# The second norm of a two-layer mixer kernel, taken segment by segment with its inverse roots as columns

## The chip, the core and the metric

The kernel runs on one core of one Trainium2 chip. The metric is the device time of one launch in microseconds (us). The core has TensorE (PE, matrix products into the eight PSUM banks; PEld is its weight load), VectorE (DVE), ScalarE (ACT), GpSimd (POOL) and SyncE (SP), which here issues all DMAs. The engines run their own instruction streams in order and meet at semaphores.

## The reference

Two layers over 512 tokens of width 2048: 256 context tokens and 256 latent tokens, whose modulation differs. Layer 0 is a gated chunk mixer with attention, layer 1 a gated delta rule in both directions. What the change touches is the residual of layer 0 and the norm of layer 1, cut to this:

```python
x = x + gate * o                    # latent tokens, layer 0
ctx = ctx + c_gate * oc             # context tokens, layer 0
h = rms_norm(x, norm_w[1]) * (1.0 + scale) + shift
hc = rms_norm(ctx, norm_w[1]) * (1.0 + c_scale) + c_shift
# rms_norm(x, w) = x * rsqrt(mean(x * x, axis=-1) + EPS) * w
qkv, z, ba = split(h @ dn_w_in)     # first products of layer 1
```

## The kernel before

Tokens lie along the free dimension: T = 512 columns, of which segment 0 (columns 0 to 255) is the context and segment 1 (256 to 511) the latent tokens. The model width is 16 k-tiles of 128 partitions. Every large product is made in fp32 quality from three fp32r products: operands are split into a rounded high part and the rest (hh and hl for the activations, wh and wl for the weights), and each k-tile takes hh x wh, hl x wh and hh x wl. Weights come in halves of 8 k-tiles (128x1024). ScalarE makes a half's high part, GpSimd its low part; SyncE loads it into one of six ring slots (layer 0, `ring`, of which the first four are `raw`) or four slots (layer 1, `raw`).

**Last output of layer 0.** PE makes 16 output tiles t (`front_tile`, L695 to L697, halves HOUT + 2t and HOUT + 2t + 1, 48 matmuls of 512 columns each) into banks 0, 1, 3, 4. DVE adds the residual for each segment (L1970, semaphore `x1_ready`), ACT squares the tile (L1346, `square`) and POOL adds the squares into `n_acc` (L2365). Tile 15 goes the same way as the others; PE then waits for POOL's last add and multiplies by a matrix of ones (`square_sum`, L679), which puts the sum over the width of each token into all 128 partitions of bank 6.

**Second norm.** ACT takes the root of 128x512 (L1350), DVE the reciprocal of 128x512 (L1814). Then DVE, ACT and DVE again work through the 16 k-tiles: scale by the inverse root (`norm_scale`, L1819, both inputs in SBUF), affine with the modulation (`norm_affine`, L1361, one operation for each segment), rounding copy to hh (`norm_hi`, L1368), and the rest to hl (`norm_lo`, L1823, both inputs in SBUF). DVE's order is scale(k), lo(k-2); ACT's is affine(k), copy(k-1). ACT makes the high parts of weight halves 0, 1 and 2 of layer 1 (`rear_split_hi`, L474) between root and first affine; POOL makes the low parts (L479) from there.

**First products of layer 1.** PE waits for both parts of weight halves 0 and 1, then for each k-tile 0 to 7 of hl makes six matmuls (halves 0 and 1, banks 0 and 4), then three for each k-tile 8 to 15 (half 2), then needs half 3 (L878 to L880). SyncE issues the loads of halves 0 and 1 when all splits of layer 0 are done, and those of 2 and later after it has sent the latent part of x to memory (`keep_x1`, L554), which waits for the last residual.

The order of the work is written out by hand on each engine; nothing is scheduled by a planner. The names that the change touches are `square_sum`, `norm_root`, `norm_inverse`, `norm_scale`, `norm_affine`, `norm_hi`, `norm_lo`, `products`, `front_half` and the split helpers.

## Time and profile before

| what | us |
|---|---|
| median of 3 runs | 2442.44 |
| lowest, highest | 2440.26, 2444.56 |
| the profiled execution | 2444.82 |
| its span on the core | 2443.0 |
| PE busy | 2337.6 (96%) |
| DVE, ACT, POOL busy | 1101.1, 1128.0, 1162.0 (45%, 46%, 48%) |

The page of the profile gives busy time by engine, the span in 40 slices, the chain of work that ended last, and the costliest groups. Times in the rows are counted from the start of the span. A matmul's duration in a row includes the drain of the array and overlaps the next one's, so what a stretch costs PE is read from the distance between starts. The granted clock (PEclk) is a share of TensorE's 2.4 GHz.

### The profile page before, as it was taken

The numbers are of one execution on the slowest core, as the hardware profiler recorded it, in microseconds if no ns is written. First come the engines' busy times: TensorE is split into PE (matmuls) and PEld (weight loads), VectorE is DVE, ScalarE is ACT, GpSimd is POOL, SyncE is SP. The second block draws the span as 40 slices with busy tenths as digits, with TensorE's granted clock in tenths as the row PEclk, the third lists the DMA queues.
The fourth block names the chain that finished last, engine by engine and source line by source line (L and its number), as shares of the span: only waits on it lengthen the run. The fifth ranks groups of instructions, "written<-read, shape, count | busy, mean of one in ns | idle before, by whom it ended". The sixth has DMA issues, their size and how long they took to land.

```text
span 2443.0 us, 59204 instructions
## 1 busy us (share of the span) xinstructions
PE 2337.6 (96%) x25854; PEld 1944.1 (80%) x25854; DVE 1101.1 (45%) x2337; ACT 1128.0 (46%) x2042; POOL 1162.0 (48%) x634
## 2 busy tenths in 40 slices
PE   6989999999999978999999999999999999998997
PEld 2557777777777856788888888888888888888997
DVE  3144443333440037655555555555555555553323
ACT  3342333323342237554665456545664466543443
POOL 2222333333335544456645664476546654563554
PEclk9999999999999989999999999999999999999998
DMA  9854555555544221233223232323222322336553
GB/s 376 318 201 178 211 212 189 190 193 190 192 181 153 95 95 45 97 114 105 97 89 109 107 108 80 106 105 113 82 103 97 119 100 81 113 103 234 187 181 117
DMA packets 99347, 352.15 MB, mean 144 GB/s; under 512 B 10768, under 2 KB 15248, under 8 KB 96784
## 3 DMA queue, kind: packets, MB, share of 16 engines
q1 hardware_dynamic: 99088, 348.36, 39.7%
q8 instruction: 204, 3.34, 0.6%
q14 instruction: 55, 0.45, 0.1%
HBM read 336.13 MB, written 12.19 MB: 143 GB/s over the span
## 4 chain that ended last, share of the span: by engine, by line
PE 82%; ACT 8%; DVE 4%; DMA 3%; issue 2%; POOL 1%; SPq 0%; ACTq 0%; DVEq 0%
PE bank L695 8%; PE bank L696 8%; PE bank L697 8%; PE bank L878 7%; PE bank L880 6%; PE bank L879 6%; PE bank L652 3%; ACT scratch L1577 3%; PE bank L918 3%; PE bank L920 2%; PE bank L919 2%; PE bank L1118 2%; PE bank L1120 2%; PE bank L1119 2%; PE bank L975 2%; PE bank L1087 2%
## 5 line engine op out<-in xcount | busy, mean ns | idle before, releaser
L479 POOL TENSOR_TENSOR wl<-raw,wh 128x1024 fp32r<-128x1024 f32 x215 | 516.6, 2410 | 623.2 <-ACT wh L474 623.2
L878 PE MATMUL bank<-hh,wh 128*128 128x512 f32 (+1 forms) x1040 | 406.8, 391 | 19.7 <-DVE hl L1823 14.9
L407 POOL TENSOR_TENSOR wl<-raw,wh 128x1024 fp32r<-128x1024 f32 x85 | 207.9, 2455 | 406.4 <-ACT wh L402 406.3
L880 PE MATMUL bank<-hh,wl 128*128 128x512 f32 (+1 forms) x1040 | 381.1, 366 | 1.1 <-issue 1.1
L879 PE MATMUL bank<-hl,wh 128*128 128x512 f32 (+1 forms) x1040 | 380.4, 366 | 1.8 <-issue 1.8
L474 ACT ACTIVATE wh<-raw 128x1024 fp32r<-128x1024 f32 x232 | 245.5, 1060 | 277.9 <-PE bank L920 121.5
L695 PE MATMUL bank<-hh,wh 128*128 128x512 f32 x864 | 346.0, 400 | 2.6 <-POOL wl L407 2.5
L697 PE MATMUL bank<-hh,wl 128*128 128x512 f32 x864 | 338.2, 391 | 0.0
L696 PE MATMUL bank<-hl,wh 128*128 128x512 f32 x864 | 338.1, 391 | 0.0
L878 PEld LDWEIGHTS bank<-hh,wh 128*128 128x128 f32 x1040 | 197.0, 189 | 55.7 <-issue 15.2
L402 ACT ACTIVATE wh<-raw 128x1024 fp32r<-128x1024 f32 x85 | 90.0, 1060 | 311.5 <-DMA raw<-w_in 191.6
L880 PEld LDWEIGHTS bank<-hh,wl 128*128 128x128 f32 x1040 | 196.9, 189 | 35.3 <-issue 2.4
L879 PEld LDWEIGHTS bank<-hl,wh 128*128 128x128 f32 x1040 | 197.7, 190 | 26.5 <-issue 1.0
L695 PEld LDWEIGHTS bank<-hh,wh 128*128 128x128 f32 x864 | 163.4, 189 | 46.0 <-issue 6.9
L696 PEld LDWEIGHTS bank<-hl,wh 128*128 128x128 f32 x864 | 163.4, 189 | 34.9 <-issue 1.9
L697 PEld LDWEIGHTS bank<-hh,wl 128*128 128x128 f32 x864 | 163.2, 189 | 34.8
L2020 DVE SCALAR_TENSOR_TENSOR scratch<-bank,sm,scratch 128x508 f32<-128x508 f32 (+3 forms) x256 | 174.0, 680 | 7.5
L918 PE MATMUL bank<-wh,hh 128*128 128x256 f32 x512 | 158.2, 309 | 3.1 <-issue 3.1
L407 POOL TENSOR_TENSOR wl<-scratch,wh 128x1024 fp32r<-128x1024 f32 x35 | 85.2, 2443 | 138.8 <-ACT wh L402 138.7
L920 PE MATMUL bank<-wh,hl 128*128 128x256 f32 x512 | 145.8, 285 | 0.0
L919 PE MATMUL bank<-wl,hh 128*128 128x256 f32 x512 | 145.6, 284 | 0.0
L975 PEld LDWEIGHTS bank<-scratch 32*32 32x32 f32 x10240 | 105.1, 104 | 33.7 <-issue 27.4
(299 smaller groups left out, 4534.0 us busy)
## 6 DMA issues: line engine op xcount, KB each, us to landing
raw<-w_in SPq DMA_DIRECT2D x259, 512.0 KB, 3.5
raw<-w_ada SPq DMA_DIRECT2D x101, 512.0 KB, 5.6
raw<-w_out SPq DMA_DIRECT2D x84, 512.0 KB, 3.6
scratch<-w_ada SPq DMA_DIRECT2D x59, 512.0 KB, 6.0
scratch<-keep_g SPq DMA_DIRECT2D x15, 1024.0 KB, 5.6
scratch<-w_in SPq DMA_DIRECT2D x23, 512.0 KB, 6.8
raw<-w_gate SPq DMA_DIRECT2D x22, 512.0 KB, 4.6
scratch<-xT SPq DMA_DIRECT2D x2, 4096.0 KB, 12.8
```

What stands on the lines that cost most here:

```text
L407: eng.tensor_tensor(fl[h % SPLIT], ring[ring_slot("half", h)], fh[h % SPLIT].bitcast(F32), ALU.subtract)\
L474: eng.activation(buffers(s)[0], raw[:, s % RAW, :], ACT.Copy).then_inc(sem("rear_hi"), 1)
L479: eng.tensor_tensor(buffers(s)[1], raw[:, s % RAW, :], buffers(s)[0].bitcast(F32), ALU.subtract)\
L695: pe.matmul(ps, w[:, k * P:(k + 1) * P], hhv[:, kk, :], start=first and k == 0, stop=False)
L696: pe.matmul(ps, w[:, k * P:(k + 1) * P], hlv[:, kk, :], start=False, stop=False)
L697: done = pe.matmul(ps, r[:, k * P:(k + 1) * P], hhv[:, kk, :], start=False, stop=last and k == HALF - 1)
L878: pe.matmul(ps, w[:, k * P:(k + 1) * P], hhv[:, kk, t0:t1], start=first and k == k0, stop=False)
L879: pe.matmul(ps, w[:, k * P:(k + 1) * P], hlv[:, kk, t0:t1], start=False, stop=False)
L880: done = pe.matmul(ps, r[:, k * P:(k + 1) * P], hhv[:, kk, t0:t1], start=False, stop=last and k == k1 - 1)
L918: pe.matmul(ps, hhv[:, k, t0:t0 + P], wk, start=(k == 0 and tt == 0), stop=False)
L919: pe.matmul(ps, hhv[:, k, t0:t0 + P], rk, start=False, stop=False)
L920: done = pe.matmul(ps, hlv[:, k, t0:t0 + P], wk, start=False, stop=(k == KT - 1 and tt == 1))
```

## The change

The last output tile, the sum of squares, the norm and the products of k-tiles 0 to 7 and 8 to 15 behind it are made for segment 0 first and for segment 1 after.

- PE makes tile 15 as 48 matmuls of 256 columns for segment 0 (bank 4) and 48 for segment 1 (bank 2). Half NHALF0 - 2 has buffers of its own (`xh`, `xl`), so that all of tile 15's weights stay.
- The sum over the width is no longer 128 equal rows: `square_columns` multiplies squares (as the stationary operand) by two columns of ones, and the sum of a token stands in a partition, a column for each 128 tokens. ACT takes the root of 128x4 (`column_root`), DVE the reciprocal of 128x4 and spreads it over the identity matrix to 128x256 (`column_inverse`), and a product with ones (`inverse_rows`) puts the inverse roots of the segment into all partitions of bank 6 or 7. POOL's last add falls away: PE adds the last tile's squares in the same bank.
- The scale reads the inverse roots from PSUM. Scale, affine, copy and rest are made in 32 steps of 128x256: k-tiles 0 to 7 for segment 0, then for segment 1, then 8 to 15 for segment 0, then for segment 1.
- Weight halves 1 and 2 are split after affine 2 and affine 8 in this sequence, half 0 ahead of the last square.
- A root of two constants is taken in the output loop (at t = 1), which loads ACT's table there.
- The loads of all four first weight halves are issued as their slots come free, ahead of the last residual.

Cut to its core, the diff:

```diff
@@ splits @@
+        def front_buffers(h):
+            return (xh, xl) if h == NHALF0 - 2 else (fh[h % SPLIT], fl[h % SPLIT])
...
@@ SyncE @@
-            sp.wait_ge(sem("front_lo"), NHALF0)
-            for s in range(2):
+            for s in range(RAW):
+                held = max(n for n in AT if n % RING == s)
+                sp.wait_ge(sem("front_lo"), AT[held][1] + 1)
                 rear_load(sp, s, w_in1[s, :, :])
...
@@ TensorE @@
+            def square_columns(s):
+                if s == 0:
+                    pe.wait_ge(sem("n_added"), ADDED)
+                pe.wait_ge(sem("n_squared"), SQUARED - 1 + s)
+                for c in range(2 * s, 2 * s + 2):
+                    cs = slice(c * P, (c + 1) * P)
+                    pe.matmul(pb[5][:, 2 * c:2 * c + 2], n_acc[:, cs], ones[:, 0:2], start=True, stop=False)
+                    done = pe.matmul(pb[5][:, 2 * c:2 * c + 2], n_sq[1][:, cs], ones[:, 0:2], start=False, stop=True)
+                done.then_inc(sem("n_summed"), 1)
+
+            def inverse_rows(s):
+                pe.wait_ge(sem("n_spread"), s + 1)
+                pe.matmul(pb[6 + s][:, SEGS[s]], ones[:, :], n_rinv[:, SEGS[s]], start=True, stop=True)\
+                  .then_inc(sem("n_summed"), 1)
...
-            square_sum()
+            front_half(h, ps[:, SEGS[0]], True, False, None, SEGS[0])
+            front_half(h + 1, ps[:, SEGS[0]], False, True, None, SEGS[0])
+            ps = pb[LASTBANK[1]]
+            pe.wait_ge(sem("mod_added"), NEARLY + 1)
+            front_half(h, ps[:, SEGS[1]], True, False, None, SEGS[1], 0, 4)
+            square_columns(0)
+            front_half(h, ps[:, SEGS[1]], False, False, None, SEGS[1], 4, HALF)
+            inverse_rows(0)
+            front_half(h + 1, ps[:, SEGS[1]], False, True, None, SEGS[1])
...
-            for k in range(HALF):
-                products(0, k, k + 1, PA[:, :], 0, T, k == 0, False, "h_lo", 0)
-                products(1, k, k + 1, pb[4][:, :], 0, T, k == 0, False, None, 0)
+            for s in range(2):
+                t0, t1 = s * SEG, (s + 1) * SEG
+                for k in range(HALF):
+                    products(0, k, k + 1, PA[:, t0:t1], t0, t1, s == 0 and k == 0, False, s, 0)
+                    products(1, k, k + 1, pb[4][:, t0:t1], t0, t1, s == 0 and k == 0, False, s, 0)
+                    if s == 0 and k == 1:
+                        square_columns(1)
+                    if s == 0 and k == 4:
+                        inverse_rows(1)
             wait_lo(pe, 2)
-            products(2, 0, HALF, PA[:, :], 0, T, False, True, "h_lo", 1)
+            products(2, 0, HALF, PA[:, 0:SEG], 0, SEG, False, False, 0, 1)
+            products(2, 0, HALF, PA[:, SEG:T], SEG, T, False, True, 1, 1)
@@ ScalarE @@
+            def column_root(s):
+                act.wait_ge(sem("n_summed"), 2 + 2 * s)
+                act.activation(n_col[:, 4 * s:4 * s + 4], pb[5][:, 4 * s:4 * s + 4], ACT.Sqrt, scale=1.0 / D,
+                               bias=eps[:, 0:1]).then_inc(sem("n_root"), 1)
...
+                if t == 1:
+                    act.activation(n_col[:, 8:10], eps[:, :], ACT.Sqrt)
+            rear_split_hi(act, 0)
+            last_square(0)
+            column_root(0)
             act.wait_ge(sem("aff_ready"), 5)
-            for s in range(3):
-                rear_split_hi(act, s)
-            norm_group(1, 0, KT // 2)
-            act.wait_ge(sem("x1_kept"), 16)
-            norm_group(1, KT // 2, KT)
+            steps = [(k, s) for k0 in (0, HALF) for s in range(2) for k in range(k0, k0 + HALF)]
+            made = segment_affine(*steps[0])
+            for j in range(1, 2 * KT):
+                if j == 2 * HALF:
+                    act.wait_ge(sem("x1_kept"), 16)
+                later = segment_affine(*steps[j])
+                segment_hi(*steps[j - 1], made)
+                made = later
+                if j == 2:
+                    rear_split_hi(act, 1)
+                if j == 4:
+                    last_square(1)
+                if j == 7:
+                    column_root(1)
+                if j == 8:
+                    rear_split_hi(act, 2)
@@ VectorE @@
+            def column_inverse(s):
+                dve.wait_ge(sem("n_root"), 2 + s)
+                ch.link(dve.reciprocal(n_col[:, 4 * s:4 * s + 4], n_col[:, 4 * s:4 * s + 4]))
+                col = n_col[:, 4 * s:4 * s + 4].rearrange("p (c o) -> p c o", o=2)[:, :, 0:1].to_broadcast([P, 2, P])
+                eye = ident.rearrange("p (c n) -> p c n", c=1).to_broadcast([P, 2, P])
+                dve.tensor_tensor(n_rinv[:, SEGS[s]].rearrange("p (c n) -> p c n", n=P), eye, col, ALU.mult)\
+                   .then_inc(sem("n_spread"), 1)
...
-            norm_inverse(1)
-            for k in range(KT):
-                norm_scale(1, k)
-                if k >= 2:
-                    norm_lo(k - 2, 1)
+            for j in range(2 * KT):
+                segment_scale(*steps[j])
+                if j >= 2:
+                    segment_lo(*steps[j - 2])
+                if j == 3:
+                    dve.wait_ge(sem("front_done"), NHALF0)
+                    first_residual(KT - 1, 1)
+                if j == 7:
+                    column_inverse(1)
+                    dve.wait_ge(sem("x1_ready"), 2 * KT)
```

How the instructions stand now. On ScalarE, between the last square and the second pair of affines, the three weight splits (`wh`) stood in a row before. In these rows `hh` is the rounded high part of the activations and `eps` the bias of the root:

```order
L1350 ACT_TABLE_LOAD
L1350 ACTIVATE scratch<-bank,eps 128x512
L474 ACTIVATE wh<-raw 128x1024 x3
L1361 ACTIVATE scratch<-scratch,mod,affa 128x256 x4
L1368 ACTIVATE hh<-scratch 128x512
L1361 ACTIVATE scratch<-scratch,mod,affa 128x256 x2
```

On ScalarE after the change, from the first weight split to square 1:

```order
L492 ACTIVATE wh<-raw 128x1024
L1401 ACTIVATE scratch<-scratch 128x256
L1410 ACTIVATE scratch<-bank,eps 128x4
L1440 ACTIVATE scratch<-scratch,mod,affa 128x256 x2
L1445 ACTIVATE hh<-scratch 128x256
L1440 ACTIVATE scratch<-scratch,mod,affa 128x256
L1445 ACTIVATE hh<-scratch 128x256
L492 ACTIVATE wh<-raw 128x1024
```

The split of half 0 moved ahead of the last square, that of half 1 behind the third affine, and the table load is gone from here.

On VectorE before, from the last residuals to the first rest (`hl`):

```order
L1970 SCALAR_TENSOR_TENSOR scratch<-bank,mod,scratch 128x256 x32
L1808 SCALAR_TENSOR_TENSOR affa<-mod,sm 128x32
L1814 RECIPROCAL scratch<-scratch 128x512
L1819 TENSOR_TENSOR scratch<-scratch 128x512 x3
L1823 TENSOR_TENSOR hl<-scratch,hh 128x512
```

On VectorE after, the same place, up to the residual of segment 1:

```order
L2072 SCALAR_TENSOR_TENSOR scratch<-bank,mod,scratch 128x256 x31
L1911 RECIPROCAL scratch<-scratch 128x4
L1914 TENSOR_TENSOR scratch<-sm,scratch 128x256
L1922 TENSOR_TENSOR scratch<-scratch,bank 128x256 x3
L1927 TENSOR_TENSOR hl<-scratch,hh 128x256
L1922 TENSOR_TENSOR scratch<-scratch,bank 128x256
L1927 TENSOR_TENSOR hl<-scratch,hh 128x256
L2072 SCALAR_TENSOR_TENSOR scratch<-bank,mod,scratch 128x256
```

The reciprocal is of four columns, the scale reads a bank, and the last residual stands behind four scales and two rests. Further on, `L1911` and `L1914` come a second time between step 7 and step 8.

## Rows read from the trace of the kernel before

**Rows 1.** The page's chain that ended last, by engine.
```profile
PE 82%; ACT 8%; DVE 4%; DMA 3%; issue 2%; POOL 1%; SPq 0%; ACTq 0%; DVEq 0%
```

**Rows 2.** Chain in order of time, 893 to 936 us: start, length, what.
```profile
894.11 0.89 DVE scratch L1970 x2
...
897.04 1.37 PE bank L679 x2
...
899.22 3.36 DVE scratch L1814
...
902.60 5.56 DVE scratch L1819 x2
...
930.78 0.61 ACT hh L1368
...
932.42 2.37 POOL wl L479
...
934.84 0.49 PE bank L878
```

**Rows 3.** Timeline of PE: start, duration, instruction, [idle before <- releaser].
```profile
739.80 0.50 PE L695 MATMUL bank<-hh,wh 128*128 128x512 f32 x1 [2.51 <-POOL wl L407]
...
910.67 0.76 PE L878 MATMUL bank<-hh,wh 128*128 128x512 f32 x1 [12.28 <-DVE hl L1823]
...
934.84 0.49 PE L878 MATMUL bank<-hh,wh 128*128 128x512 f32 x1 [1.51 <-POOL wl L479]
```

**Rows 4.** Timeline of ACT behind the norm.
```profile
909.19 0.61 ACT L1368 ACTIVATE hh<-scratch 128x512 fp32r<-128x512 f32 x1
909.71 1.08 ACT L1361 ACTIVATE scratch<-scratch,mod,affa 128x256 f32<-128x256 f32 x2
...
912.19 0.62 ACT L1368 ACTIVATE hh<-scratch 128x512 fp32r<-128x512 f32 x1
```

**Rows 5.** Timeline of DVE behind the norm.
```profile
909.83 0.69 DVE L1823 TENSOR_TENSOR hl<-scratch,hh 128x512 fp32r<-128x512 f32 x1 [1.08 <-ACT hh L1368]
910.44 0.68 DVE L1819 TENSOR_TENSOR scratch<-scratch 128x512 f32<-128x512 f32 x1
```

**Rows 6.** Timeline of PE, products of 256 columns in layer 1.
```profile
940.98 0.28 PE L879 MATMUL bank<-hl,wh 128*128 128x256 f32 x1
941.10 0.28 PE L880 MATMUL bank<-hh,wl 128*128 128x256 f32 x1
```

**Rows 7.** Timeline of ACT, narrow operations.
```profile
957.03 0.42 ACT L1591 ACTIVATE scratch<-scratch 128x256 f32<-128x256 f32 x1 [2.87 <-DVE scratch L2020]
...
970.66 0.20 ACT L1616 ACTIVATE scratch<-scratch 128x4 f32<-128x4 f32 x1
```

**Rows 8.** Timeline of PE, two fp32 products of two columns.
```profile
964.00 0.51 PE L945 MATMUL bank<-ones,scratch 128*128 128x2 f32 x4
```

**Rows 9.** Timeline of DVE, 256-wide tensor_tensor with and without a bank.
```profile
939.14 2.50 DVE L1993 TENSOR_TENSOR scratch<-scratch 128x256 f32<-128x256 f32 x1
...
944.18 0.42 DVE L1996 TENSOR_TENSOR scratch<-scratch 128x256 f32<-128x256 f32 x1
...
950.76 0.42 DVE L2247 TENSOR_TENSOR scratch<-bank,scratch 128x256 f32<-128x256 f32 x1
```

**Rows 10.** Chain, four fp32 products of 256 columns.
```profile
233.71 1.73 PE bank L788 x8
```

**Rows 11.** Timeline of POOL beside rows 9.
```profile
936.55 4.81 POOL L479 TENSOR_TENSOR wl<-raw,wh 128x1024 fp32r<-128x1024 f32 x2 [1.77 <-ACT wh L474]
...
946.58 4.68 POOL L479 TENSOR_TENSOR wl<-raw,wh 128x1024 fp32r<-128x1024 f32 x2 [2.89 <-ACT wh L474]
```

**Rows 12.** Windows: length, busy by engine, granted clock, DMA share, GB/s.
```profile
741.20:744.00 2.80, 2.80 (x8) 2.12 (x8) 0.00 (x0) 0.00 (x0) 2.80 (x2) 0.50 0.91 331
897.80:898.20 0.40, 0.40 (x1) 0.00 (x0) 0.00 (x0) 0.00 (x0) 0.00 (x0) 0.51 1.07 381
935.40:936.40 1.00, 1.00 (x8) 0.86 (x7) 0.13 (x2) 1.00 (x3) 0.00 (x0) 1.00 0.69 123
```

More of the change, by code:

```diff
@@ L554, in _ @@
             sp.dma_start(keep_x1, xv[:, :, SEG:T]).then_inc(sem("x1_kept"), 16)
-            for s in range(2, 12):
+            for s in range(RAW, 12):
                 rear_load(sp, s, w_in1[s, :, :])
@@ L685, in first_square_sum, with front_half @@
                 pe.matmul(pb[6][:, :], ones[:, :], n_odd, start=False, stop=True).then_inc(sem("n_summed"), 1)
-            def front_half(h, ps, first, last, ready=None):
+            def front_half(h, ps, first, last, ready=None, ts=slice(0, T), k0=0, k1=HALF):
                 pe.wait_ge(sem("front_lo"), h + 1)
-                w, r = fh[h % SPLIT], fl[h % SPLIT]
-                for k in range(HALF):
+                w, r = front_buffers(h)
+                for k in range(k0, k1):
                     kk = (h % 2) * HALF + k
@@ L881, in products @@
                                      stop=last and k == k1 - 1)
-                if k1 == HALF:
+                if k1 == HALF and ready != 0:
                     done.then_inc(sem("rear_done"), 1)
@@ L1356, in norm_affine @@
+            def norm_affine(k):
+                act.wait_ge(sem("n_scaled"), k + 1)
                 if k >= 8:
-                    act.wait_ge(sem("h_lo"), layer * KT + k - 8 + 1)
-                full = norm_full(layer, k)
+                    act.wait_ge(sem("h_lo"), k - 8 + 1)
                 for s in range(2):
-                    m = layer * 3 * KT + k
-                    last = act.activation(full[:, s * SEG:(s + 1) * SEG], norm_t(layer, k)[:, s * SEG:(s + 1) * SEG],
-                                          ACT.Identity, scale=affa[:, k, s:s + 1], bias=mod[:, m, s:s + 1])
-                    made = ch.mark(last)
+                    made = ch.mark(act.activation(norm_full(0, k)[:, SEGS[s]], norm_t(0, k)[:, SEGS[s]],
+                                                  ACT.Identity, scale=affa[:, k, s:s + 1], bias=mod[:, k, s:s + 1]))
@@ L1364, in norm_affine, with norm_hi, norm_group @@
                 return made
[L1366 removed]
+            def norm_hi(k, made):
                 ch.wait(made)
[L1368 to L1371 removed]
+                act.activation(hhv[:, k, :], norm_full(0, k), ACT.Copy).then_inc(sem("h_hi"), 1)
+            def norm_group(first, end):
+                made = norm_affine(first)
@@ L1372, in norm_group, with segment_affine @@
                 for k in range(first + 1, end):
-                    later = norm_affine(layer, k)
-                    norm_hi(layer, k - 1, made)
+                    later = norm_affine(k)
+                    norm_hi(k - 1, made)
                     made = later
-                norm_hi(layer, end - 1, made)
+                norm_hi(end - 1, made)
+            def segment_affine(k, s):
+                act.wait_ge(sem("n_scaled"), KT + order1(k, s) + 1)
+                if k >= HALF:
+                    act.wait_ge(sem("h_lo"), KT + order1(k - HALF, s) + 1)
+                return ch.mark(act.activation(norm_full(1, k)[:, SEGS[s]], norm_t(1, k)[:, SEGS[s]], ACT.Identity,
+                                              scale=affa[:, k, s:s + 1], bias=mod[:, 3 * KT + k, s:s + 1]))
@@ L2376, in _ @@
                     add_squares(k)
-            for k in range(KT - 3, KT):
+            for k in range(KT - 3, KT - 1):
                 add_squares(k)
```

160 lines of the change are left out of this document (95 added, 65 removed).

## The prediction

> **What bounds the kernel now.** I read the page's chain of waits first: TensorE carries 82% of it and ScalarE 8% [rows 1], so a change that leaves the big products alone can only win where TensorE stands still. The chain in order of time shows one such place, between the last output tile of the first layer and the first product behind the second norm [rows 2]. There the tile's last matmul ends at 894.1 us; residual, squares, sum and root follow; the reciprocal of 128x512 takes 3.36, two scalings take 5.56, and TensorE gets its next product at 910.67, after 12.28 us idle behind the ones-matmul [rows 3]. From then on it is not TensorE that sets the pace: the affine and the rounding copy on ScalarE do, one k-tile every 1.50 us (909.19 to 912.19 is two) [rows 4], until the last copy at 930.78. Behind it come ScalarE's split of the fourth weight half, GpSimd's 2.37 us, and the product at 934.84 [rows 2]. **934.84 is the mark**: what follows is the same in both kernels and TensorE-bound, so the change is worth what it moves that start. Everything ahead of tile 15 keeps its time (the GpSimd adds and the splits of halves 118 and 119 come no later than before).
>
> **Why 1.50.** VectorE takes its steps in turn: scale(k), lo(k-2), scale(k+1), lo(k-1). So lo waits for the copy, the next scale stands behind lo, the next affine waits for that scale, and the next copy for the affine. From the rows: copy 0.61, hand-over 0.04, lo until the next may start 0.61, scale 0.68 and hand-over 0.09, affine of two halves until the copy may start 0.98: 3.01 for two k-tiles, as measured [rows 4, 5]. ScalarE's own work is also 2 x (0.98 + 0.52) = 3.00, so before the change the loop costs nothing extra.
>
> **The change, part by part.** Times are those of the profiled run.
>
> Tile 15 in two segments: 48 matmuls of 256 columns start 0.12 apart [rows 6], so 5.8 us for each segment, 11.5 for both where 48 of 512 (0.227 apart) took 10.9. The tile began at 883.0 (its end at 894.1 less 10.9 and a tail of 0.2), so segment 0 is ready at 889.0.
>
> First chain, segment 0: residual 0.48 (half of 0.89 [rows 2]) and square 0.42 [rows 7] end at 889.9. TensorE takes four fp32 column products when its 12 queued matmuls are out, at 890.2: two of them took 0.51 [rows 8], so 0.9. Root 0.20 [rows 7], the four-column reciprocal below that, spread 0.42 [rows 9]: 892.0. TensorE has 12 more matmuls queued until 892.4, then the 256-column ones-product; four such took 1.73 [rows 10], one 0.43 plus its tail: 893.0. The first scale is 0.42, and the **first affine starts at 893.5**. What is taken out is the 3.36 reciprocal and the two slow scalings.
>
> First product: TensorE must have both weight halves 0 and 1 (it waits for both ahead of k = 0). Half 1 is split on ScalarE after three affines and two copies (2.1 us), 1.05 itself, then 2.37 on GpSimd: TensorE starts at **899.3**, 11.4 earlier. Its own tile ends at 895.9 (883.0, 11.5 for the 96 matmuls, 1.2 for column and ones-products between them, tail 0.2), so it idles 3.4.
>
> The loop behind the norm, 32 steps of 256 columns. Half the width is not half the time: a 256-wide ScalarE operation takes 0.42 against 0.61 [rows 4, 7], a VectorE one 0.42 against 0.69 [rows 5, 9]. ScalarE's own work is 0.49 + 0.31 = 0.80 a step (0.31 worked out from 0.52 and the 0.21 less that the narrow one takes). The loop is 0.41 + 0.04 + 0.35 + 0.43 + 0.06 + 0.49 = 1.78 for two steps. **It now binds**: 0.89 a step, 1.78 for a k-tile where it was 1.50. Bounds: 0.80 (only ScalarE's work counts) and 1.10 (each hand-over 0.2 dearer, as TensorE's first matmul after a wait is [rows 3]); I take 0.89, since the same sum gives 3.01 before.
>
> What stands in the loop besides: (a) GpSimd's split of weight half 1. A 256-wide tensor_tensor with both inputs in SBUF took 2.50 beside GpSimd's split and 0.42 alone, one with an input in PSUM 0.42 beside it [rows 9, 11]; so the scales (inverse roots in PSUM) pass and the lo's stand until the split ends. With 0.95 for ScalarE's split and 0.31 for square 1 it puts affine 7 at 901.7 instead of 899.7 (GpSimd's split lies at 896.7 to 899.1, lo 2 ends behind it, scale 5 and affine 5 follow at 899.5 and 899.9): 2.0. (b) The turn to segment 1: behind affine 7 and copy 6 come root 1 at 902.5, reciprocal and spread until 903.4, the ones-product until 904.1 and scale 8; affine 8 at 904.6 is 2.9 after affine 7, 2.0 more than a step. (c) Weight half 2 is split at step 8, on ScalarE until 906.4 and on GpSimd until 908.9; lo 8 stands, and affine 11 comes at 909.7 instead of 907.2: 2.5. Before, the three splits lay under the reciprocal. Bounds: ScalarE's part alone (1.3 and 1.0) to both engines' splits in full (3.6 and 3.3).
> The Trainium skill's page "SBUF — State Buffer", section "Who interferes with whom", has the same exemption for a VectorE instruction with at most one SBUF input, as a rule. If PSUM-fed scales stood too, the sum would be 0.2 longer.
>
> TensorE's clock. Two idles, of 2.51 us [rows 3] and of 2.9 (894.1 to 897.04 [rows 2]), were followed by a fall of the granted clock within a microsecond of the next matmul: 0.50 in 741.2 to 744.0, 0.51 from 897.8 [rows 12], that is from 2.4 to 1.2 GHz, for about 3.4 us at the first place. After 1.51 us idle [rows 3] it stayed 1.00 [rows 12]. The new idle of 3.4 is longer than both that brought a fall. From about 899.6 the half clock then lengthens the five steps of segment 0 and the column products that stand ahead of ones-product 1 (4.3 us at full clock) by 1.7: the turn to segment 1 costs 3.7 instead of 2.0.
>
> **Sum.** 893.5 + 31 steps x 0.89 (27.6) + 2.0 + 3.7 + 2.5 + 0.8 (last copy behind the last affine) = 930.1 for the last copy, against 930.78. Then 0.3 until ScalarE may go on, split 1.05, GpSimd 2.37, hand-overs 0.2: **934.0 against 934.84, a gain of 0.8**. So of the 11 to 15 us won at the front of the stage, ScalarE and VectorE give back nearly all: from the affine at 908.2 (902.60 + 5.56) to the last copy they took 22.6 us, wide and with the splits behind them, and from 893.5 they take 36.6. The profiled run took 2444.82 us with a span of 2443.0, 2.4 above the median; the gain is a difference inside it and goes onto the median: 2442.44 - 0.8 = **2441.6**.
>
> **Rivals.**
> - *The loop does not bind* (faster). If VectorE kept ahead and the lo's stood beside nobody, only ScalarE's work would count: 893.5 + 31 x 0.80 + 2.3 (two splits, square, root) + 0.3 = 920.9, mark 924.8, gain 10.0: 2432.4. Against it: the order on VectorE, and [rows 9, 11]. Halfway (loop at 0.80, the rest as summed) gains 3.6. Chance 0.17 for a gain over 4.9, whole or in part.
> - *No fall of the clock at 899.6*: 1.7 less, gain 2.5, 2439.9. For it: the fall has not come behind every idle, and where it comes is not tied to the matmul. Chance 0.15.
> - *A second fall behind the last idle*. TensorE ends its products at 931.7 and waits 2.3 for GpSimd, between 1.51 (no fall) and 2.51 (fall). What follows is TensorE-bound, so 3.4 us at half clock cost 1.7: 2443.3. Chance 0.13.
> - *Every hand-over dearer* (slower). A narrow step has a semaphore wait on each engine; if the loop took 2.18 instead of 1.78, 16 pairs cost 6.4 more: mark 940.4, 5.6 late, 2448.0. It decides from 2.14 a pair. Against it: 3.01 from the same terms. Chance 0.10.
> - *Nothing of a narrow step overlaps* (same). If ScalarE's 0.59 + 0.42 stood end to end, a step would take 1.01 and the stage 3.7 more: 2445.3. Against it: an affine is followed after 0.49 by the next operation in the two-half rows [rows 4]. Chance 0.04. The Trainium skill's page "VectorE: DVE Perf Modes", section "The TRN2 errata", states this as a rule: both engines pay a fixed latency between instructions, and operands of 512 elements or more are advised.
> - That the change does not do what it says is ruled out by the order of instructions: both segments' work and both ones-products are there, and ScalarE loads no table between square and root.
>
> **How the numbers follow.** The forecast itself has 0.41; with the two clock cases and the steps end to end 0.73 lies within 0.2% (4.9 us, about what a measurement can tell), 0.17 faster, 0.10 slower. The range 2435.5 to 2446.5 leaves out the whole of the first rival and the dear hand-over, and takes in the halfway gain, both clock cases and the steps end to end.
>
> **What the profile after would show.** First affine near 893.5 and first product near 899.3: if either is 2 us off, the first chain or the split of half 1 is mis-sized. Copies in pairs 1.78 apart in the second half of the stage: 1.6 there means the first rival. VectorE lo's of 2 us beside both GpSimd splits. Granted clock 0.5 at 900 to 903. Last copy near 930.1 and the mark near 934.0. Segment 1's first scale near 905.9; near 904.1 if the clock holds. I am wrong in kind if the last copy comes before 925 or after 935.

## The result, and the profile after

The changed kernel took 2454.3 us, median of 4 runs (2453.0 to 2457.9), against 2442.4 us (2440.3 to 2444.6) of the kernel before: a ratio of 1.0053, 95% interval 1.0040 to 1.0065. It is slower, by 12 us where a gain of 0.8 was forecast, and outside the range. The profiled execution has a span of 2453.5 us against 2443.0.

The first rows are from the page of the changed kernel: TensorE's busy time and instructions, the instruction fetches by queue (packets, MB), and the chain that ended last by engine. They answer to [rows 1].

```profile
span 2453.5 us, 59546 instructions
...
PE 2348.2 (96%) x25992; PEld 1959.1 (80%) x25992; DVE 1100.2 (45%) x2372; ACT 1131.5 (46%) x2061; POOL 1161.0 (47%) x633
...
q8 instruction: 205, 3.36, 0.6%
...
PE 83%; ACT 8%; DVE 3%; DMA 3%; issue 3%; POOL 1%; SPq 0%; ACTq 0%; DVEq 0%
```

"issue" has 3% of the chain: TensorE, ready in every way that the profile shows, stands still. Keep that line in mind.

**The changed stage went about as forecast.** The timeline of the changed kernel, from several cuts (start, duration, engine, line, operation, idle time before it and its releaser): the first matmul of tile 15, the first affine, the first product, the lo that stands beside GpSimd's split, segment 1's first scale, the last copies, and the mark.

```profile
880.99 0.28 PE L725 MATMUL bank<-hh,scratch 128*128 128x256 f32 x1
...
891.73 1.09 ACT L1440 ACTIVATE scratch<-scratch,mod,affa 128x256 f32<-128x256 f32 x2 [2.29 <-DVE scratch L1922]
...
897.39 0.36 PE L920 MATMUL bank<-hh,wh 128*128 128x256 f32 x1 [3.43 <-POOL wl L497]
...
905.72 0.42 DVE L1922 TENSOR_TENSOR scratch<-scratch,bank 128x256 f32<-128x256 f32 x1 [3.52 <-PE bank L708]
...
908.86 1.88 DVE L1927 TENSOR_TENSOR hl<-scratch,hh 128x256 fp32r<-128x256 f32 x1 [0.98 <-ACT hh L1445]
...
928.94 0.71 ACT L1445 ACTIVATE hh<-scratch 128x256 fp32r<-128x256 f32 x2
...
933.08 0.79 PE L920 MATMUL bank<-hh,wh 128*128 128x512 f32 x1 [2.24 <-POOL wl L497]
```

Everything ahead of tile 15 ended 2.0 us earlier in this execution (881.0 for 883.0). The change did not do this: 1.85 us of it are there by 253 us, and the first instruction that it adds, the root of two constants, runs at 738.6. Add it back, and the first affine is at 893.7 (forecast 893.5), the first product at 899.4 (899.3), segment 1's first scale at 907.7 (905.9, the one term that is 1.8 off), the mark at 935.1 (934.0; before 934.84, [rows 2]). So the stage ends 0.2 later instead of 0.8 earlier.

**The loss is behind it.** Layer 1 works through 16 heads. These rows are the second group of eight value products of the first, second and fifteenth head; the time of a head is that from the row before it to its own, so that the times below begin with the second head, and the "head stretch" goes from the first row to the fifteenth. Changed kernel, then the kernel before:

```profile
1070.45 1.16 PE L1179 MATMUL bank<-scratch 128*128 128x128 f32 x8
...
1153.65 1.16 PE L1179 MATMUL bank<-scratch 128*128 128x128 f32 x8
...
2195.33 1.16 PE L1179 MATMUL bank<-scratch 128*128 128x128 f32 x8
```
```profile
1067.22 1.16 PE L1137 MATMUL bank<-scratch 128*128 128x128 f32 x8
...
1148.02 1.16 PE L1137 MATMUL bank<-scratch 128*128 128x128 f32 x8
...
2184.92 1.16 PE L1137 MATMUL bank<-scratch 128*128 128x128 f32 x8
```

From the second head on they take 83.2, 82.0, 81.6, 80.9 and then 79.6 us; before they took 80.8, 80.3, 79.8, 79.7, 79.6. The whole account of the 10.5 us: -2.0 ahead of tile 15, +0.2 in the stage, +5.0 from the mark to the first of these rows (132.4 before, 137.4 after), **+7.2 in the head stretch** (1117.7 before, 1124.9 after), +0.1 behind it. In these heads the two kernels have the same instructions in the same order.

**Where it is lost.** Both timelines of TensorE in the second head, at the same place: a burst of 128 tiny matmuls, then wide products. Changed kernel:

```profile
1092.93 1.29 PE L1017 MATMUL bank<-scratch 32*32 32x32 f32 x122 [0.42 <-ACT scratch L1730]
1096.19 0.33 PE L1017 MATMUL bank<-scratch 32*32 32x32 f32 x6 [1.97 <-issue]
1096.45 0.80 PE L920 MATMUL bank<-hh,wh 128*128 128x512 f32 x1
```

Kernel before:

```profile
1089.71 1.49 PE L975 MATMUL bank<-scratch 32*32 32x32 f32 x128 [0.42 <-ACT scratch L1647]
1091.13 0.50 PE L878 MATMUL bank<-hh,wh 128*128 128x512 f32 x1
...
1092.16 0.40 PE L879 MATMUL bank<-hl,wh 128*128 128x512 f32 x1
1093.47 0.39 PE L880 MATMUL bank<-hh,wl 128*128 128x512 f32 x1 [0.91 <-issue]
```

After the change the burst is torn: 122 matmuls, 1.97 us of nothing, the last 6. Before, all 128 pass, then 5 wide ones, and then there is 0.91 us of nothing. The place has moved by 6 + 5 = 11 matmuls.

The +5.0 ahead of these heads has the same look. The first head's burst is torn in the changed kernel for 2.12 us, behind an earlier wait of 0.81; the kernel before waits once, 1.79, so the waits make 1.1 of the 5.0. Changed kernel, then the kernel before:

```profile
1012.83 0.28 PE L1017 MATMUL bank<-scratch 32*32 32x32 f32 x10 [2.12 <-issue]
```
```profile
1011.74 0.39 PE L879 MATMUL bank<-hl,wh 128*128 128x512 f32 x1 [1.79 <-issue]
```

The rest is about what the clock can have cost. From the mark to the first head row (changed kernel, then the kernel before: start:end, length, busy time, matmuls, granted clock, DMA share, GB/s) the granted clock is 0.95 against 0.99, which by an estimate from these two windows is up to 5.5 us of full speed; the changed kernel ran at half clock right behind the mark and again behind the torn burst, where the kernel before did not.

```profile
933.08:1070.45 137.37, 128.79 (x1550) 0.95 0.29 95
```
```profile
934.84:1067.22 132.38, 124.41 (x1551) 0.99 0.28 98
```

**What ends there.** The queue q8 brings TensorE's instructions: 204 transfers of 16.4 KB before, 205 after. Each of TensorE's matmuls is a weight load and a multiplication; with 2 x 25992 of these and 537 waits of its own, the changed kernel has 52521 instructions, 256 in each transfer. (The Trainium skill, "Advanced Engine Details and Errata", section "ISA Cache", gives the same 16 KB and 256 instructions; the trace agrees.) Counted along TensorE's program, each of these waits in layer 1 stands at a multiple of 256 from the one before, in both kernels. It holds for every run of this document: the fourteen profiles have 116 waits of TensorE of 0.8 us or more with "issue" as releaser, all at the same place of the 256 to within one instruction, and each ends 1.2 to 1.6 us after a fetch of q8 has landed. The change added 138 matmuls and 2 waits: 278 instructions, that is 256 and 22. So every end of a piece behind the stage lies 22 instructions, 11 matmuls, earlier in the work. A head has 2560 instructions, exactly ten pieces, so the ends fall at the same places of every head.

The windows of TensorE (start:end, length, busy time, matmuls, granted clock, DMA share, GB/s) and the transfers in two of them show why it waits there and hardly anywhere else:

```profile
1087.70:1091.00 3.30, 3.30 (x140) 1.00 0.10 36
1091.00:1094.00 3.00, 2.58 (x127) 1.00 0.00 0
1094.00:1096.19 2.19, 0.22 (x23) 0.97 0.03 7
1096.19:1107.00 10.81, 10.81 (x106) 0.85 0.47 148
```
```profile
DMA packets 0, 0.00 MB, mean 0 GB/s; under 512 B 0, under 2 KB 0, under 8 KB 0
...
q8 instruction: 2, 0.03, 3.0%
```

From 1087.7 to 1094.0 two whole pieces are used up, in 3.3 and 3.0 us. The next transfer is not seen at all from 1091.0 to 1093.9 (first line of the second fence, no packet of any kind); two come in 1094.0 to 1098.6 (second line), and the first takes 1.0. The one that TensorE waits for starts at 1094.04, 5.4 us behind the fetch before it, lands at 1095.0, and TensorE goes on at 1096.19. Between 950 and 2200 us there are 151 fetches, and no two of them start less than 3.4 us apart; the two pieces were used up faster than that. The least distance is not the whole story, though: a fetch 3.4 us behind its predecessor would have started at 1092.0. What held it back for 2 us more is not shown. Where TensorE has only wide products, 0.23 us each, a piece lasts far longer (up to 24.5 us from one fetch to the next) and the fetch is hidden. (The Trainium skill, "Runtime: NRT & Kernel Launch", section "Instruction fetch mechanics", has the fetch as hidden since an engine issues more slowly than it is filled. Here that holds for the wide products and not for the bursts.) The clock adds to it: 0.85 in the window behind the wait, and the wide products, 0.23 apart at 2.4 GHz, follow 0.43 apart at 1.2.

### The profile page after: what moved, and what is told of

The parts are those of the page before. It is cut to its first block, busy times and chain, and to the rows that moved or that the text cites. A ratio compares the mean times of both kernels' runs of the same rounds, so it can differ in the third digit from the quotient of the medians.

```text
span 2453.5 us, 59546 instructions
## 1 busy us (share of the span) xinstructions
PE 2348.2 (96%) x25992; PEld 1959.1 (80%) x25992; DVE 1100.2 (45%) x2372; ACT 1131.5 (46%) x2061; POOL 1161.0 (47%) x633
## 4 chain that ended last, share of the span: by engine, by line
PE 83%; ACT 8%; DVE 3%; DMA 3%; issue 3%; POOL 1%; SPq 0%; ACTq 0%; DVEq 0%
PE bank L725 8%; PE bank L727 8%; PE bank L726 8%; PE bank L920 7%; PE bank L922 7%; PE bank L921 7%; PE bank L671 3%; PE bank L1017 3%; PE bank L961 2%; PE bank L960 2%; PE bank L962 2%; ACT scratch L1660 2%; PE bank L1160 2%; PE bank L1162 2%; PE bank L1161 2%
## 5 line engine op out<-in xcount | busy, mean ns | idle before, releaser
L920 PE MATMUL bank<-hh,wh 128*128 128x512 f32 (+1 forms) x1064 | 416.2, 391 | 16.6 <-POOL wl L497 8.6
L922 PE MATMUL bank<-hh,wl 128*128 128x512 f32 (+1 forms) x1064 | 387.7, 364 | 1.6 <-issue 1.6
L921 PE MATMUL bank<-hl,wh 128*128 128x512 f32 (+1 forms) x1064 | 387.4, 364 | 0.0
L725 PE MATMUL bank<-hh,wh 128*128 128x512 f32 (+1 forms) x864 | 344.4, 399 | 2.5 <-POOL wl L423 2.5
L727 PE MATMUL bank<-hh,wl 128*128 128x512 f32 (+1 forms) x864 | 336.2, 389 | 0.0
L726 PE MATMUL bank<-hl,wh 128*128 128x512 f32 (+1 forms) x864 | 335.9, 389 | 0.0
L920 PEld LDWEIGHTS bank<-hh,wh 128*128 128x128 f32 x1064 | 204.3, 192 | 51.3 <-POOL wl L497 9.7
L922 PEld LDWEIGHTS bank<-hh,wl 128*128 128x128 f32 x1064 | 204.1, 192 | 32.7
L921 PEld LDWEIGHTS bank<-hl,wh 128*128 128x128 f32 x1064 | 205.0, 193 | 27.4 <-issue 2.7
L725 PEld LDWEIGHTS bank<-hh,wh 128*128 128x128 f32 x864 | 163.4, 189 | 44.7 <-POOL wl L423 7.1
L726 PEld LDWEIGHTS bank<-hl,wh 128*128 128x128 f32 x864 | 163.5, 189 | 34.3 <-issue 1.9
L727 PEld LDWEIGHTS bank<-hh,wl 128*128 128x128 f32 x864 | 163.0, 189 | 34.2
L423 POOL TENSOR_TENSOR wl<-scratch,wh 128x1024 fp32r<-128x1024 f32 x34 | 82.9, 2446 | 139.0 <-ACT wh L418 138.9
## 6 DMA issues: line engine op xcount, KB each, us to landing
scratch<-xT SPq DMA_DIRECT2D x2, 4096.0 KB, 12.7
```

What stands on the lines that cost most here:

```text
L423: eng.tensor_tensor(front_buffers(h)[1], ring[ring_slot("half", h)], front_buffers(h)[0].bitcast(F32), ALU.subtract).then_inc(sem("front_l ...
L725: pe.matmul(ps, w[:, k * P:(k + 1) * P], hhv[:, kk, ts], start=first and k == 0, stop=False)
L726: pe.matmul(ps, w[:, k * P:(k + 1) * P], hlv[:, kk, ts], start=False, stop=False)
L727: done = pe.matmul(ps, r[:, k * P:(k + 1) * P], hhv[:, kk, ts], start=False, stop=last and k == HALF - 1)
L920: pe.matmul(ps, w[:, k * P:(k + 1) * P], hhv[:, kk, t0:t1], start=first and k == k0, stop=False)
L921: pe.matmul(ps, w[:, k * P:(k + 1) * P], hlv[:, kk, t0:t1], start=False, stop=False)
```

## The experiments

The theory ("position"): the time depends on where the ends of the pieces fall in the bursts, and not on what the change does in the norm. The rivals: the stage, its clock falls or the idle time that it no longer has; and, in the second set, TensorE's last idle time ahead of the mark. "Place" below is how many instructions earlier the pieces end than in the kernel before, behind the stage (a minus: later).

**Moving the pieces alone.** Edits of the first two, ahead of the first product behind the norm and ahead of the first matmul of the program (two waits in a row become one instruction):

```diff
+            for _ in range(44):
+                pe.wait_ge(sem("consts"), 1)
             wait_lo(pe, 0)
```
```diff
+            for _ in range(512):
+                pe.wait_ge(sem("consts"), 1)
             pe.wait_ge(sem("small_in"), 16)
```

> The kernel before, unchanged but for 22 instructions more on TensorE's queue (waits on a semaphore that has long been reached), put into its idle time of 12.28 us ahead of the first product after the norm. TensorE's instructions come in pieces of 256; the change added 278 = 256 + 22, so from here on the pieces end where they end in the changed kernel. Theory 'position' (the head loop lost its time because the ends of the pieces moved against the loop's bursts of small matmuls): +6 to +9 us over the kernel before, the first four heads of layer 1 about 83, 82, 81.5, 81 us instead of 80.8, 80.3, 79.8, 79.7. Rival 'stage' (the changed stage, its clock falls or its missing idle time, left the loop worse off): no change, within 1 us.

Measured: ratio 1.0048 (1.0033 to 1.0063), 2455.1 us. Nothing was added but 22 waits in idle time, and the kernel before became as slow as the changed one; the loss of 11 us is more than the 6 to 9 expected. Heads of 84.9, 83.1, 81.4, 80.8 us; head stretch 1126.4. In the second head, at the changed kernel's place:

```profile
1096.16 0.33 PE L975 MATMUL bank<-scratch 32*32 32x32 f32 x6 [2.52 <-issue]
```

> The kernel before with 256 such waits more on TensorE's queue at the start of the program, ahead of its first matmul, which waits 16 us for its first transfer. The pieces end in the same places as before, one piece later. Theory 'position': no change, within 1 us, heads of layer 1 as before. Rival 'more instructions cost by their number': as much as the 22 cost or more.

Measured: ratio 1.0049 (1.0034 to 1.0064), 2455.0 us: not the "no change" that was expected. The trace tells the two apart. The first matmul comes at 29.1 us instead of 16.3, since 256 waits take longer than the idle time they stand in (they follow each other 0.106 us apart), and 10.4 of these 12.8 us are still there at the end. The head stretch is 1116.8, 0.9 less than before, with heads of 80.5, 79.8, 79.6, 79.8. The pieces do nothing when moved by a whole one; the 256 waits cost their own time at the start.

The third has the same edit with a smaller number:

```diff
+            for _ in range(256):
+                pe.wait_ge(sem("consts"), 1)
             pe.wait_ge(sem("small_in"), 16)
```

> The kernel before with 128 such waits more at the start: the pieces end half a piece away from where they end in the kernel before, in every stage. Theory 'position': a different time, by 1 to 8 us in either direction, with TensorE's waits in layer 1's heads at other places of the burst. Rival 'stage': no change, within 1 us.

Measured: ratio 1.0132 (1.0115 to 1.0148), 2474.2 us. The 30 us are far outside the 1 to 8 expected. Here the first three of the times are 79.5 us each, with no wait; from the fourth time on they are 81.4 to 83.1, with up to three waits of 0.8 to 2.0 us each, and the head stretch is 1144.7.

And in the changed kernel:

```diff
+            for _ in range(468):
+                pe.wait_ge(sem("consts"), 1)
             pe.wait_ge(sem("small_in"), 16)
```

> The changed kernel with 234 such waits more at the start of TensorE's queue: behind the changed stage the pieces end where they end in the kernel before (22 + 234 = 256). Theory 'position': about 2446 us, 7 to 9 us under the changed kernel, with heads of layer 1 near 80.8, 80.3, 79.8, 79.7 us; what is left over the kernel before is the clock's second fall of about 3 us. Rival 'stage': it stays at 2454 us and the heads at 83.2, 82.0, 81.6, 80.9 us.

Measured: ratio 1.0035 (1.0021 to 1.0049), 2452.7 us, and not the 2446 expected. Against the kernel before, the first matmul is 10.5 late and the end 12.7 by the profile, so most of the total is again the waits themselves. The head stretch is 1117.2 against 1124.9 of the changed kernel: as expected, heads of 80.9, 80.3, 79.6, 79.6. From the first matmul of tile 15 to the end of the span it takes 1560.5 us; the kernel before takes 1560.0, the changed kernel 1572.6. The total could not show it; the stretches do.

**The changed kernel at other places, without waits at the start.** Products for both segments at once save 3 matmuls a block: fewer instructions, same work.

```diff
-            products(2, 0, HALF, PA[:, 0:SEG], 0, SEG, False, False, 0, 1)
-            products(2, 0, HALF, PA[:, SEG:T], SEG, T, False, True, 1, 1)
+            products(2, 0, 4, PA[:, 0:SEG], 0, SEG, False, False, 0, 1)
+            products(2, 0, 4, PA[:, SEG:T], SEG, T, False, False, 1, 1)
+            products(2, 4, HALF, PA[:, :], 0, T, False, True, 1, 1)
```

> The changed kernel with TensorE's program 22 instructions shorter behind the stage, so that the pieces of 256 end where they do in the kernel before, and nothing moved at the start: the last four blocks of the second half are multiplied for both segments at once (12 matmuls fewer, 24 instructions), and 2 waits on a reached semaphore are added. Theory 'position': the heads of layer 1 take what they take before (80.8, 80.3, 79.8, 79.7 us), the stretch from the first head mark to the last loses nothing against before, and the kernel comes to about 2446 us (2454.3 less 7 to 8). Rival 'the heads are slow for something else in the stage': 2454 us, heads 83.2, 82.0, 81.6, 80.9.

Measured: **2442.8 us** (10 runs) against 2443.9 of the kernel before beside it, ratio 1.0000 (0.9985 to 1.0015). Twenty-two instructions fewer take the whole loss away, 3 us more than expected. Heads 81.1, 80.1, 79.6, 79.8, head stretch 1118.0. The wait of the second head is back among the wide products:

```profile
1093.00 0.40 PE L922 MATMUL bank<-hh,wl 128*128 128x512 f32 x1 [1.19 <-issue]
```

**The clock's second fall and the last idle time.** In the profile after, the clock did fall behind the mark, and not in the same stretch before [rows 12]. The next two take that idle time away, by an earlier split and by ten matmuls in it.

```diff
                 if j == 8:
                     rear_split_hi(act, 2)
+                if j == 29:
+                    rear_split_hi(act, 3)
             segment_hi(*steps[-1], made)
-            rear_split_hi(act, 3)
```

> The changed kernel with the fourth weight block of the second layer split before the last copies of the loop (in front of the copy of step 28 of 0 to 31) and not behind them; TensorE's program as long as in the changed kernel. TensorE's last idle time ahead of the mark is 2.24 us there. If that idle time brings the clock's second fall: idle under 1.5 us, the mark about 1 us earlier, no fall behind it, together 3 to 4 us less (2451 us). If the fall comes from the narrow products before it, or if the split only pushes the loop back: within 1 us of the changed kernel. The heads stay as slow as in the changed kernel by the theory 'position'.

Measured: ratio 1.0069 (1.0049 to 1.0089), 2459.1 us, where the changed kernel has 1.0053 (1.0040 to 1.0065): no gain. The idle time wandered into the loop:

```profile
931.79 0.58 PE L920 MATMUL bank<-hh,wh 128*128 128x256 f32 x1 [2.19 <-DVE hl L1928]
```

VectorE's lo's stood beside GpSimd's split there, as the prediction has it for the other splits, and the mark came no earlier: 52.4 us behind the first matmul of tile 15, 52.1 in the changed kernel.

```diff
+            for _ in range(10):
+                pe.matmul(pb[6][:, :], xh[:, 0:P], hhv[:, 0, :], start=True, stop=True)
             wait_lo(pe, 3)
```

> The changed kernel with ten matmuls more, 128x512, 0.22 us each at the full clock, into a bank that nobody reads then, in TensorE's last idle time of 2.24 us ahead of the mark; the last four blocks of the second half for both segments at once and 4 waits more bring the pieces of 256 back to where they end in the changed kernel. If the idle time brings the clock's fall at the mark: no fall there, from the mark to 17 us behind it 15.2 us and not 18.0, and so about 2451.5 us, with heads as slow as in the changed kernel. If the fall was on its way before that idle time: no change, 2454 us.

Measured: ratio 1.0067 (1.0049 to 1.0085), 2458.4 us. The windows of TensorE behind the mark, changed kernel and then this one:

```profile
936.00:940.00 4.00, 4.00 (x13) 0.62 0.55 148
```
```profile
936.00:940.00 4.00, 4.00 (x21) 1.00 0.43 131
```

The fall is gone and the total is no better; the heads are as slow as in the changed kernel (stretch 1125.8). The test is not a clean one for the clock: GpSimd's split ends at 935.5 and the ten matmuls only at 936.2, the mark comes 53.7 us behind the first matmul of tile 15 instead of 52.1, and the way from the mark to the first head row falls from 137.4 to 134.5. It is a clean one for the position: this run has the same four wide blocks as the run at place 0, but its pieces end at +22, and it is slow. So what helped there was not that the blocks were wide.

The ten matmuls once more, now at place 0: the last two blocks of the first half are wide besides the four of the second, and there are 12 waits in the text:

```diff
+            for _ in range(12):
+                pe.wait_ge(sem("consts"), 1)
             wait_lo(pe, 0)
```

> Both together: ten matmuls in the last idle time, and TensorE's program brought to 256 instructions over that of the kernel before (the last two blocks of the first half and the last four of the second for both segments at once, and 6 waits). Theory 'position' with the clock's fall as the rest: 2454.3 less 8 and less 2.8, 2443 to 2444 us, equal to the kernel before. If the two losses aren't separate ones, it stays above 2448 us.

Measured: 2442.9 us, ratio 1.0004 (0.9993 to 1.0014). It is at the kernel before, as expected, but so is the run at place 0 without the ten matmuls: nothing in the totals asks for a second loss. That the clock's fall costs nothing is not shown, since here GpSimd's split ends at 933.6 and the ten matmuls hold the mark back to 935.8.

**How far it goes.** Widening more blocks moves the pieces' ends later than in the kernel before; 64 waits in the kernel before move them earlier. Two blocks of the first half, besides the four of the second:

```diff
-                for k in range(HALF):
+                for k in range(HALF - 2 if s == 0 else HALF):
+                    if k == HALF - 2:
+                        t0 = 0
```

> The changed kernel with TensorE's program 48 instructions shorter behind the stage: 230 more than before, so that the pieces of 256 end 26 instructions (13 matmuls) later in every burst than in the kernel before (the last two blocks of the first half and the last four of the second for both segments at once). Theory 'position': the wait in the second head's burst fell from 2.16 us to 1.31 us by the 11 matmuls between the changed kernel and the kernel before; 13 more take it under 1 us, so the heads are at least as fast as before, and the kernel comes to 2439 to 2443 us, at or under the kernel before. Rival 'any shift away from before costs, as +22 and +128 did': 2450 us or more.

Measured: 2440.7 us, ratio 0.9990 (0.9979 to 1.0002). Heads 79.6 from the first on, stretch 1115.1: the pieces end 13 matmuls later and the wait of the second head is gone; the only one of 0.8 us or more left is in the last head (2.94).

Seven blocks of the second half instead of four:

```diff
-            products(2, 4, HALF, PA[:, :], 0, T, False, True, 1, 1)
+            products(2, 1, HALF, PA[:, :], 0, T, False, True, 1, 1)
```

> The changed kernel with TensorE's program 66 instructions shorter behind the stage: 212 more than before, the pieces end 44 instructions (22 matmuls) later than in the kernel before (the last two blocks of the first half and all but the first of the second for both segments at once). Theory 'position': no wait in the bursts of the heads 1 to 4, unless the end of the piece before it now falls into the burst's fast part; 2438 to 2446 us. The blocks of the second half for both segments at once make TensorE wait longer for the first of them, up to 1 us at the mark. Rival 'any shift costs': 2450 us or more.

Measured: **2438.9 us** (9 runs) against 2442.8, ratio 0.9979 (0.9968 to 0.9991): the fastest of all, and faster than the kernel before by 0.2%. The kernel before was not run at this place, so how much of this is the place and how much the changed stage is open. The burst that was torn:

```profile
1088.07 1.34 PE L1017 MATMUL bank<-scratch 32*32 32x32 f32 x128 [0.42 <-ACT scratch L1733]
1089.34 0.50 PE L920 MATMUL bank<-hh,wh 128*128 128x512 f32 x1
```

Its heads are 79.5, 79.5, 79.6, 79.7; two late heads wait (1.27 and 1.59 at 2111 and 2122 us), so that the stretch is 1117.4, as in the kernel before. What it wins by the profile lies outside: 1.4 us from the mark to the first head row (131.0 for 132.4) and 3.3 from the fifteenth head row to the sixteenth (61.1 for 64.4), where its longest wait is 1.64 us and the kernel before has 3.10, the changed kernel 4.58.

The kernel before, with the loop of the first experiment longer:

```diff
-            for _ in range(44):
+            for _ in range(128):
```

> The kernel before with 64 waits on a reached semaphore more in TensorE's 12.28 us of idle time, as the 22 of the first experiment: the pieces end 32 matmuls earlier in the bursts. Theory 'position': slower than the kernel before, as both +22 (11 us) and +128 (30 us) are, so 2450 to 2475 us; whatever its size, the waits stand at an end of a piece. Rival 'the loss is a loss of the idle time in front of the loop': 2444 us, as none of this idle time is on the chain.

Measured: ratio 1.0109 (1.0089 to 1.0129), 2467.9 us, head stretch 1142.6. The waits again stand in the bursts, in more heads:

```profile
1427.40 0.31 PE L975 MATMUL bank<-scratch 32*32 32x32 f32 x11 [1.73 <-issue]
...
1511.35 0.33 PE L975 MATMUL bank<-scratch 32*32 32x32 f32 x7 [2.55 <-issue]
```

And the changed kernel with four blocks of the first half wide, the rest as at -44:

```diff
-                for k in range(HALF - 2 if s == 0 else HALF):
-                    if k == HALF - 2:
+                for k in range(HALF - 4 if s == 0 else HALF):
+                    if k == HALF - 4:
                         t0 = 0
```

> The changed kernel with TensorE's program 90 instructions shorter behind the stage: 188 more than before, the pieces end 68 instructions (34 matmuls) later than in the kernel before (the last four blocks of the first half and all but the first of the second for both segments at once; the ones-product of the second segment one block earlier). By the runs so far the time falls from +64 over +22, 0 and -26 to -44: 24, 11, 0, -3 and -5 us against before. Theory 'position': the time depends on where the ends of the pieces fall in the burst, so this goes on only until the end of the piece before, 128 matmuls earlier, moves into the part of the burst that +64 and +22 showed to be bad; it is 128 - 34 = 94 matmuls ahead of the end at before's place, while +64 is 32 and +128 is 64 ahead of it. 2433 to 2445 us if 94 is still outside, 2450 or more if it is inside. The stage itself costs up to 1 us more at the mark.

Measured: 2444.6 us, ratio 1.0008 (0.9997 to 1.0020). The first ten times are 79.6 or 79.7, but from 1875 us on TensorE waits where two ends of pieces fall into bursts, with 19 and with 31 of 128 matmuls still to come. The ends lie there in the earlier heads too, without a wait of 0.8 us. The second of them:

```profile
1881.23 0.45 PE L1017 MATMUL bank<-scratch 32*32 32x64 f32 x31 [1.58 <-issue]
```

The head stretch is 8.5 us longer than in the kernel before and the total the same, since 2.1 us are won from the mark to the first head row (130.3) and 4.3 from the fifteenth head row to the sixteenth (60.0).

In one table:

| place | kernel | ratio to before | head stretch, us |
|---|---|---|---|
| -68 | changed, more blocks wide | 1.0008 | 1126.2 |
| -44 | changed, more blocks wide | 0.9979 | 1117.4 |
| -26 | changed, more blocks wide | 0.9990 | 1115.1 |
| 0 | before | 1 | 1117.7 |
| 0 | changed, four blocks wide | 1.0000 | 1118.0 |
| +22 | changed | 1.0053 | 1124.9 |
| +22 | before and 22 waits | 1.0048 | 1126.4 |
| +64 | before and 64 waits | 1.0109 | 1142.6 |
| +128 | before and 128 waits | 1.0132 | 1144.7 |

At both places where both kernels were run, 0 and +22, they agree within the intervals, so that the norm shows in neither. Beyond +22 only the kernel before was run, below 0 only the changed one.

## Why the prediction was wrong

- **The step that failed** is the sentence on the mark: "what follows is the same in both kernels and TensorE-bound, so the change is worth what it moves that start". The instructions behind the mark are the same, but their numbers in TensorE's program are not, and by its number an instruction waits for its fetch or doesn't. Adding 22 instructions to the kernel before cost 11 us; taking them off the changed kernel gave the 11 us back. None of the rivals had it. Their one slow case priced a loop of dearer hand-overs, and that did not happen.
- **The hint was there before.** The kernel before has the same waits, 1.79 us in its first head, 0.91 in its second and 3.10 in its last, with "issue" as releaser. "issue" has 2% of the chain before [rows 1], and the prediction says nothing of it. These waits are not fixed when a change adds or takes TensorE instructions ahead of them.
- *First chain and first product*: right, within 0.2 us.
- *The loop, 1.78 for two steps*: 1.73 measured (affines 0.85 and 0.89 apart). Right.
- *GpSimd's splits stop VectorE's lo's*: right, 1.88 us for one of 0.42 at 908.86, and seen again when the fourth split was moved.
- *The turn to segment 1*, with the clock: 1.8 too small for the scale at 905.72. The prediction took 3.4 us at half clock, costing 1.7; the window below shows 6.6 at half clock, and the 4.3 us of work ahead of the ones-product took 7.6, from 897.39 to 905.01. A loop of 1.73 instead of 1.78 gave back 0.7 of the 1.8 by the end: the mark is at +0.2 where -0.8 was forecast. The medians at equal place put the stage at 0 within 4 us, so that neither number is shown by them.

```profile
898.20:904.80 6.60, 6.60 (x33) 0.50 1.00 355
```

- *A second fall of the clock behind the last idle* (a rival with 0.13): it happened, 0.62 in 936 to 940, in the profile, and is part of the +5.0. The 12 us do not need it: the kernel before with 22 waits has the same total with a granted clock of 1.00 in 936 to 940, right behind its mark. What the fall costs by itself is not shown.
- *The sum* of 2441.6 us is in reach of what the changed kernel takes once the pieces lie as before, 2442.8 measured, with four blocks wide. That run was even with the kernel before to within 3.7 us, so a gain of 0.8 is neither shown nor ruled out.

**What stays open.** Why the waits fade after four of the times at +22, and set in only at the fourth at +128 and at the eleventh at -68. The ends of the pieces are at the same matmuls in each head; what moves is the time that TensorE needs for the 256 ahead of the torn burst (3.2 us in the second head of the changed kernel, 5.2 at the same place in the sixth), and no run here separates what sets that. What starts a fetch is not shown either: those that ended the 116 waits started 3.4 to 9.2 us behind the fetch before (and one 36 us), most of them 5 to 6. And the prices of the position and of the clock's falls that come with it were not taken apart.

## What to carry to other kernels

Where the chain of waits has "issue" on TensorE inside bursts of tiny matmuls, count the instructions that a change adds ahead of them, weight loads included, and take them modulo 256: in this case the shift decided more than the change did. Before judging a change worth under 1%, try it at two or three shifts, best by making a few matmuls wide or narrow where there is slack and not by waits at the start, which took 0.106 us each and were only free as long as TensorE had idle time for them (128 were, 256 were not). And compare stretches of the trace, not totals alone: with 256 waits more the total said the opposite of what the stretch shows.

## What the runs showed of the hardware

- TensorE's instruction fetches start 3.24 us apart at the least in these traces; at the torn burst of the second head 256 instructions were used up in 3.0 us. Each of the 116 waits ended 1.2 to 1.6 us after a fetch had landed; they took 0.8 to 2.6 us in the first fifteen heads, and up to 5.7 in the last (run with ten matmuls, +22). Behind the waits of 2.12 and 1.97 us in the changed kernel the granted clock was at half.
- 22 waits on a semaphore reached long before, in idle time, cost 11 us of 2443 through their number alone; 256 more at the start left the head stretch as it was (1116.8 for 1117.7).
- An early split of a weight half by GpSimd beside VectorE's last steps made the last three 256-wide lo's take 2.55 us together (0.42 is one alone), and TensorE's idle time of 2.24 us ahead of the mark came back as 2.19 ahead of its last narrow products.
